# A decoder layer on one core: head factors a head ahead, a batched last norm, a separate buffer for the third group's maxima, and an expert product moved ahead of four transposes

## The reference, cut to what matters

```
u = x * (1 + sc1) + sh1                      # sc1, sh1, ... = silu(c) @ w_ada + b_ada, six rows of 1024
z = u @ w_in                                 # the columns of all branches, split below
y_gla = gla(q, k, v, r, lr @ w_gate)         # 4 heads, 8 chunks of 64 tokens: b = cumsum(log a);
    att   = (q exp(b - ref)) (k exp(ref - b))^T, masked
    state = state * exp(b_last) + (k exp(b_last - b))^T v
    o     = att v + (q exp(b)) state ; o = rms_norm(o) * norm_g * silu(r)
y_att = three groups of dilated attention (8 heads each, head size 64), softmax per group,
        groups merged by their maxima and sums
x1 = layer_norm(alpha * x + g1 * (merge(y_gla, y_att) @ w_out))
u2 = x1 * (1 + sc2) + sh2
y  = top-1 group, top-2 of 32 SwiGLU experts on u2
out = layer_norm(alpha * x1 + g2 * y)
```

## Time and profile before

| what | value |
| --- | --- |
| median of three runs | 1498.01 us |
| the profiled execution: its time, its span | 1499.82 us, 1497.5 us |
| mean granted TensorE clock | 0.932 |
| busy PE, DVE, ACT, POOL | 88%, 69%, 46%, 23% |
| chain that ended last, by engine | PE 79%, DVE 11%, ACT 3%, DMA 2%, SPq 2%, issue 2% |
| linear attention heads, from the first `gp` to the first `yT` transpose | 189.7 to 383.0 us |
| first expert product to the last | 871.1 to 1452.0 us |
| after the last product | 1452.0 to 1497.5 us |

### The profile page before, as it was taken

How to read it: one execution, slowest core, us unless ns; L and a number is a source line. 1 busy time by engine, 2 the same in 40 slices (tenths; PEclk the granted TensorE clock), 3 DMA queues, 4 the chain that set the end, 5 groups by cost and what they waited for, 6 DMA issues and landing times.

```text
span 1497.5 us, 18092 instructions
## 1 busy us (share of the span) xinstructions
PE 1318.7 (88%) x6280; PEld 1069.7 (71%) x6280; DVE 1032.6 (69%) x1144; ACT 690.0 (46%) x844; POOL 351.0 (23%) x212
## 2 busy tenths in 40 slices
PE   3899976886899997999989469999999999999970
PEld 2678764554689887888768458888888888888850
DVE  6755855445344332343779768999999999999957
ACT  2322233123333332445230337777767777777721
POOL 0000000000000000000000133655556555655430
PEclk8899988977999998999999579999999999999985
DMA  9965321101220313225341949999999999999922
GB/s 351 334 238 218 120 85 42 43 1 41 72 70 27 115 57 114 70 71 183 124 163 74 405 162 353 372 373 363 366 378 352 372 379 370 375 372 358 355 80 112
DMA packets 73970, 318.63 MB, mean 213 GB/s; under 512 B 14978, under 2 KB 15138, under 8 KB 49088
## 3 DMA queue, kind: packets, MB, share of 16 engines
q1 hardware_dynamic: 57728, 284.41, 51.2%
q0 software_dynamic: 15328, 30.39, 6.5%
q10 hardware_dynamic: 864, 3.15, 0.5%
HBM read 315.67 MB, written 31.04 MB: 232 GB/s over the span
## 4 chain that ended last, share of the span: by engine, by line
PE 79%; DVE 11%; ACT 3%; DMA 2%; SPq 2%; issue 2%; DVEq 0%; POOLq 0%; ACTq 0%
PE ps L931 12%; PE ps L933 12%; PE ps L932 12%; PE ps L725 10%; PE ps L726 10%; PE ps L727 10%; PE ps L852 2%; PE ps L921 2%; PE ps L894 1%; PE ps L810 1%; PE ps L830 1%; PE ps L827 1%; PE ps L818 1%; PE ps L948 1%; PE ps L864 1%
## 5 line engine op out<-in xcount | busy, mean ns | idle before, releaser
L1607 DVE TENSOR_TENSOR w_lo<-w_raw,w_hi 128x2048 fp32r<-128x2048 f32 x192 | 433.2, 2285 | 41.0 <-ACT w_hi L1134 41.0
L1134 ACT CAST w_hi<-w_raw 128x2048 fp32r<-128x2048 f32 x192 | 357.6, 1919 | 0.0
L931 PE MATMUL ps<-w_hi,xT_hi 128*128 128x512 f32 x512 | 207.5, 405 | 2.4 <-DVE xT_lo L1620 2.4
L664 POOL DMA_INDIRECT y_d<-yb,ui x32 | 162.7, 5084 | 171.9 <-DVE yb L1615 147.5
L933 PE MATMUL ps<-w_hi,xT_lo 128*128 128x512 f32 x512 | 201.7, 394 | 0.0
L932 PE MATMUL ps<-w_lo,xT_hi 128*128 128x512 f32 x512 | 200.7, 392 | 0.0
L1222 DVE TENSOR_TENSOR d_lo<-d_raw,d_hi 128x1024 fp32r<-128x1024 f32 x96 | 115.1, 1222 | 82.4 <-ACT d_hi L1002 81.8
L725 PE MATMUL ps<-uT_hi,d_hi 128*128 128x512 f32 x384 | 156.0, 406 | 1.3 <-DVEq L1272 1.2
L727 PE MATMUL ps<-uT_hi,d_lo 128*128 128x512 f32 x384 | 151.4, 394 | 0.0
L726 PE MATMUL ps<-uT_lo,d_hi 128*128 128x512 f32 x384 | 151.2, 394 | 0.0
L933 PEld LDWEIGHTS ps<-w_hi,xT_lo 128*128 128x128 f32 x512 | 96.9, 189 | 21.7
(11 more groups left out here) (304 smaller groups left out, 2201.4 us busy)
## 6 DMA issues: line engine op xcount, KB each, us to landing
w_raw<-in SPq DMA_DIRECT2D x192, 1024.0 KB, 7.4
d_raw<-in SPq DMA_DIRECT2D x96, 512.0 KB, 3.3
ada_buf<-in SPq DMA_DIRECT2D x8, 2048.0 KB, 10.4
ada_w<-in SPq DMA_DIRECT2D x8, 1024.0 KB, 14.0
att_d<-Og POOLq DMA_DIRECT2D x2, 1056.0 KB, 7.4
O<-att_d POOLq DMA_DIRECT2D x2, 1056.0 KB, 8.0
x_in<-in SPq DMA_DIRECT2D x1, 2048.0 KB, 13.8
brep_d<-bvec_d POOLq DMA_DIRECT2D x2, 1024.0 KB, 18.6
```

What stands on the lines that cost most here:

```text
L664: pool.indirect_dma_start(y_d, bass.IndirectOffsetOnAxis(ap=idxs[s], axis=0), yb[s][:, :], None, bounds_check=S - 1, oob_is_err=False, com ...
L931: pe.matmul(dst, a_hi[:, k, :], hi[:, w], start=(k == 0), stop=False)
L1134: act.copy(w_hi[n % NHI][:, :], w_raw[j][:, :]).then_inc(w_hi_rdy, 1)
L1607: dve.tensor_tensor(w_lo[j][:, :], w_raw[j][:, :], w_hi[n % NHI][:, :].bitcast(f32), ALU.subtract).then_inc(w_lo_rdy, 1)
```

## The change

Five things are done.

1. **Head factors.** `gla_args` is cut in two: the arguments (`gla_args`) and the exponentials with their four products (`gla_fac`). Head 0's stand among the `ra` blocks (after blocks 17 and 20 of 24); those of head h+1 stand in head h, the arguments between `gla_kv` and `gla_o`, the factors behind `gla_o`. One block lies between `gla_kv` and `gla_o`, two behind. To clear the memory that the arguments use, the modulation sums take blocks 1 to 16 and their loads come earlier.
2. **Third group.** Its maxima and sums go to a buffer `stat2`; only ACT's first `PV` of the group waits for the store of the second, and DVE copies `stat2` into `Og[1]` at the end.
3. **Experts.** In the first stage the gate product of chunk 1 stands ahead of the transposes of h of chunk 0, with the splits that it needs ahead too.
4. **y_d.** `y_d` starts as alpha times x1 (ACT scales the first norm's gain and bias), so the zero stores, the separate x1 store and its load at the end are gone.
5. **Tail.** No addition; statistics of all four tiles first, one rsqrt for the four; DVE finishes three tiles with two operations each; ACT and POOL (two products, L700 and L701 of the changed kernel) finish the fourth.

```diff
     for n, o in enumerate(sum(gla_q, [])):
-        if n and n % 4 != 2 and halves:
+        if n and halves:
...
+        if n == 17:
+            z(("gp", 0, None))
+            steps.append(("gla_args", 0))
+        if n == 20:
+            steps.append(("gla_fac", 0))
     for h in range(GH):
-        z(("gp", h, None))
-        steps.append(("gla_args", h))
-        zs_next(g0[3 * h]), zs_next(g0[3 * h + 1])
         steps.append(("gla_kt", h))
         steps.append(("gla_kv", h))
-        zs_next(g0[3 * h + 2])
+        if h + 1 < GH:
+            z(("gp", h + 1, None))
+            steps.append(("gla_args", h + 1))
+        zs_next(g0[3 * h])
         steps.append(("gla_o", h))
+        if h + 1 < GH:
+            steps.append(("gla_fac", h + 1))
+        zs_next(g0[3 * h + 1]), zs_next(g0[3 * h + 2])
...
-        ada_after = {11: (2,), 13: (3,), 15: (4,), 19: (5, 6), 23: (7,)}
+        ada_after = {10: (2,), 12: (3,), 14: (4,), 15: (5, 6), 19: (7,)}
...
-            pool.dma_start(x1_d[P * t:P * t + P, :], x1[:, t, :]).then_inc(x1_st, 16)
+            pool.dma_start(y_d[P * t:P * t + P, :], x1[:, t, :]).then_inc(x1_st, 16)
...
-        for t in range(NT):
-            pool.dma_start(y_d[P * t:P * t + P, :], xg[1][:, :]).then_inc(y_zero, 16)
...
+        pool.wait_ge(xn_rdy, 1)
+        r = ya[:, NT - 1, :]
+        link(pool.tensor_tensor(r, r, ln2gb[:, 0, :], ALU.mult))
+        pool.tensor_tensor(r, r, ln2gb[:, 1, :], ALU.add).then_inc(last_rdy, 1)
...
                 down(n + 2, i)
-            h_transposes(c)
+                h_transposes(c)
             if not final:
...
                 product(bank(0), xT_hi[1 - s], xT_lo[1 - s], n + 4, i)
+                if first:
+                    h_transposes(c)
...
+            if kind == "wo" and q == 0:
+                act.wait_ge(ln_used, 1)
+                act.mul(ln_g[:, :], ln_g[:, :], ALPHA).then_inc(ln_alpha, 1)
+                act.mul(ln_b[:, :], ln_b[:, :], ALPHA).then_inc(ln_alpha, 1)
...
-                if j == 0 and g == 2:
-                    act.wait_ge(att_st[0], 16)
...
-                                          bias=nmx[a % 2][:, t:t + 1], accum_out=og[:, t, j, DH + 1:DH + 2])
+                                          bias=nmx[a % 2][:, t:t + 1],
+                                          accum_out=stat2[:, 1, t, j:j + 1] if g == 2 else og[:, t, j, DH + 1:DH + 2])
...
                 act.wait_ge(pv_ps, a + 1)
+                if a == 2 * HPG:
+                    act.wait_ge(att_st[0], 16)
...
             if first:
-                todo = [5, 6, 7, 8]
+                todo = [6, 7, 8]
             sigmoid(c)
+            if first:
+                x_split(c + 1, 1 - s)
...
-                if j == 0 and g == 2:
-                    dve.wait_ge(att_st[0], 16)
...
+            elif kind == "PV" and a == 3 * HPG - 1:
+                dve.wait_ge(p_sb, 3 * HPG)
+                dve.wait_ge(att_st[0], 16)
+                dve.tensor_copy(Og[1][:, :, :, DH:DH + 2].rearrange("p t h c -> p c t h"), stat2[:, :, :, :]).then_inc(stat_rdy, 1)
...
-            link(dve.scalar_tensor_tensor(out=r, in0=x1b[:, t, :], scalar=ALPHA, in1=ya[:, t, :], op0=ALU.mult, op1=ALU.add))
-            row_stats(r, rs4[:, t:t + 1])
...
+            dve.bn_stats(bn4[:, 12 * t:12 * t + 6], ya[:, t, 0:512])
+            link(dve.bn_stats(bn4[:, 12 * t + 6:12 * t + 12], ya[:, t, 512:1024]))
+            link(dve.bn_aggr(mv4[:, 2 * t:2 * t + 2], bn4[:, 12 * t:12 * t + 12]))
...
+        rsqrt(rs4, ssq, rs_t)
...
+        for t in range(NT - 1):
+            r = ya[:, t, :]
+            link(dve.scalar_tensor_tensor(out=r, in0=r, scalar=mv4[:, 2 * t:2 * t + 1], in1=ln2gb[:, 0, :],
+                                          op0=ALU.subtract, op1=ALU.mult))
+            dve.scalar_tensor_tensor(out=r, in0=r, scalar=rs4[:, t:t + 1], in1=ln2gb[:, 1, :],
+                                     op0=ALU.mult, op1=ALU.add).then_inc(fin_rdy, 1)
```

More of the change, by code:

```diff
@@ L539, in _ @@
         sp.dma_start(ln2gb[:, 1, :], ln2_b.broadcast_to([P, D])).then_inc(ln2_in, 16)
-        sp.wait_ge(w_used, NRAW * last + (NRAW + 4))
-        sp.dma_start(x1b[:, :, :], x1_d.rearrange("(t p) d -> p t d", p=P)).then_inc(x1_back, 16)
         sp.wait_ge(w_used, NRAW * last + (NRAW + 6))
@@ L546, in _ @@
             sp.dma_start(ya[:, t, :], y_d[P * t:P * t + P, :]).then_inc(fin_in[t], 16)
+        sp.wait_ge(fin_rdy, 2)
+        sp.dma_start(out[P:2 * P, :], ya[:, 1, :]).then_inc(out_st, 16)
+        sp.wait_ge(last_rdy, 1)
+        sp.dma_start(out[P * NT - P:P * NT, :], ya[:, NT - 1, :]).then_inc(out_st, 16)
     @block.gpsimd
@@ L667, in _ @@
         gather(0, 0)
-        pool.wait_ge(y_zero, 16 * NT)
+        pool.wait_ge(x1_st, 16 * NT)
         gather(1, 1)
@@ L1151, in stage @@
             if first:
-                todo = [5, 6, 7, 8]
+                todo = [6, 7, 8]
             sigmoid(c)
+            if first:
+                x_split(c + 1, 1 - s)
             for m in todo[:2]:
                 w_split(m, i)
-            if not final:
+            if not first and not final:
                 x_split(c + 1, 1 - s)
@@ L1175, in _ @@
         w_split(4, 0)
+        w_split(5, 0)
         x_split(0, 0)
@@ L1192, in _ @@
             act.dma_start(ya[:, t, :], y_d[P * t:P * t + P, :]).then_inc(fin_in[t], 16)
-        for t in range(NT):
-            act.wait_ge(nmr_rdy, t + 1)
-            act.activation(r2[:, t, :], r2[:, t, :], ACT.Identity, bias=nmr[:, t:t + 1], scale=rs4[:, t:t + 1]).then_inc(xn_rdy, 1)
-            if t:
-                act.wait_ge(fin_rdy, t)
-                act.dma_start(out[P * t - P:P * t, :], r2[:, t - 1, :]).then_inc(out_st, 16)
-        act.wait_ge(fin_rdy, NT)
-        act.dma_start(out[P * NT - P:P * NT, :], r2[:, NT - 1, :]).then_inc(out_st, 16)
+        act.wait_ge(nmr_rdy, 1)
+        t = NT - 1
+        act.activation(ya[:, t, :], ya[:, t, :], ACT.Identity, bias=nmr[:, t:t + 1], scale=rs4[:, t:t + 1]).then_inc(xn_rdy, 1)
+        for t in (0, 2):
+            act.wait_ge(fin_rdy, t + 1)
+            act.dma_start(out[P * t:P * t + P, :], ya[:, t, :]).then_inc(out_st, 16)
         act.wait_ge(out_st, 16 * NT)
@@ L1296, in evac @@
                     dve.tensor_tensor(mods[:, 1, :], lnt[0][:, :], mods[:, 1, :], ALU.add)
-                    link(dve.tensor_tensor(mods[:, 2, :], ln_g[:, :], mods[:, 2, :], ALU.mult))
+                    dve.tensor_tensor(mods[:, 2, :], ln_g[:, :], mods[:, 2, :], ALU.mult).then_inc(ln_used, 1)
+                    dve.wait_ge(ln_used, 1)
                     dve.wait_ge(out_rdy, i + 1)
@@ L1628, in stage @@
             if first:
-                todo = [5, 6, 7, 8]
-            for m in todo[:2]:
+                todo = [None, None, None, 6, 7, 8]
+            for m in todo[:2] if not first else []:
                 w_rest(m, i)
@@ L1633, in stage @@
                 x_rest(c + 1, 1 - s)
-            for m in todo[2:3]:
+            for m in todo[2:3] if not first else []:
                 w_rest(m, i)
@@ L1655, in _ @@
         w_rest(4, 0)
+        w_rest(5, 0)
         stage(0, 0, first=True)
```

43 lines of the change are left out of this document (21 added, 22 removed).

## The result

The changed kernel takes 1420.45 us (median of 4 runs, 1416.15 to 1420.77), the kernel before 1498.32 beside it: a ratio of 0.9473, with a 95% interval of 0.9456 to 0.949. Forecast were 1419.6 us. The profiled execution has a span of 1418.7 us (1497.5 before).

What follows compares the result with a forecast made beforehand. PE was taken to bound nearly all of the span, through its waits, its lower clock and the tail. Gains of 50.3 + 9.1 + 5.3 + 13.7 = 78.4 us from 1498.0 gave 1419.6 us, range 1405 to 1438.

Steps and rivals of the forecast that it cites:

- the 5 us added for the clock: Heads: 5 us added to the section's time in case light small products alone make PE's clock fall.
- the middle of 2.1 and 4.2 us: Heads, small products L810: time taken midway, as nothing showed whether clock or issue limits them.
- the bounds of 38 and 58: Heads: gain at least 38 us with slow L810 and a fall in each, at most 58 with fast L810, none.
- the clock term: Third attention group: one fall of PE's clock, 1.6 us, gained besides the wait of 7.5 us.
- DVE's three tiles, two operations of 1.25 each, 7.5: Tail: DVE finishes three tiles with two operations of 1.25 us each, 7.5 us in all.
- the third rival: Tail: POOL and DVE take turns, POOL's time coming on top of DVE's; 1424 to 1425 us, chance 0.15.
- POOL's guessed 5.8 us: Tail: time of POOL's two products, 2.9 us each, taken as three fills.
- The 0.3 us guessed for scalars read from memory: Tail: 0.3 us more for DVE's operations on its three tiles, whose scalars are read from memory.
- The likeliest case: Whole kernel: the summed gains hold, 1412 to 1428 us around the forecast, chance 0.45.
- Modulation loads late: Rival, `ra` section: waits move there through a late load or DVE behind at every block; 1436 us, chance 0.08.
- A steady loop with a new wait: Rival, experts: a wait for DVE in every chunk; at 3 us a chunk 1513 us, slower, chance 0.02.
- The clock falling in every head: Rival, heads: the clock falls in each and L810 stays at 4.2 us; gain 38, time 1432 us, chance 0.15.

## Why the prediction was right, point by point

- **Part 1, 50.3 forecast, 55.6 measured.** Its steps held nearly to the microsecond: the last `ra` block ends at 199.6 (199.8), head 0's state products at 204.8 (205.5), the three heads take 98.1 (97.7), the rest to `yT` 24.65 (24.5). The mis-sized term is the 5 us added for the clock. I feared that light products alone make it fall; in the heads it fell only behind the waits of 4.68 and 2.58 us. The first had its own 1.6 in the `ra` section; the second cost 1.7 that the heads' sum had not counted, and got back from L810, taken as the middle of 2.1 and 4.2 us and measured at 2.46, 0.7 less in each head. So L810 hung mostly on the clock. Between the bounds of 38 and 58 this part came out near the upper one. Outside the heads, something like the fear did happen: in the second attention group the clock fell behind small products with a wait of only 0.60 us, at 3.2 us in this execution and 1.6 in the second one. That the small products are the cause is not shown, since the same ones left the clock at 1.00 before.
- **Part 2, 9.1 forecast.** The 8.3 between the marks of the table hold the fall just named. From marks around the place it gained 10.4, and 9.1 by undoing it. The wait is as forecast (7.5, 7.3); the clock term, forecast at 1.6, was 2.9 and 1.8.
- **Part 3, 5.3 forecast.** 4.9 between marks, 4.4 to 5.2 by undoing it. The new wait for `hb` is 2.1, not 3. The gain lasted to the tail, as the earlier trace rows had let expect.
- **Part 4, 0 forecast.** No difference.
- **Part 5, 13.7 forecast, 10.1 measured.** The step that failed is "DVE's three tiles, two operations of 1.25 each, 7.5": DVE's six take 11.7 us (1403.69 to 1415.35), because POOL's products take turns with it. This is the mechanism of the third rival. Its price was too high: it put POOL's guessed 5.8 us on top of DVE's, but the products alone are 2.33 each and 4.0 us came on top. The 0.3 us guessed for scalars read from memory came out as 0.2 in the sum (1.28 an operation against 1.25). The likeliest case held in heads, group and experts and this rival in the tail; the chance of 0.15 for it was too low, since both sides were known to read two tensors in SBUF at once. The page "GPSIMD Engine Reference" of the Trainium skill had the better answer twice. Its section 3.1 puts a `tensor_tensor` add on GpSimd at 1.96 times VectorE's time; the trace agrees, since 2.33 against 1.22 is 1.9. Its section 8 names contention with VectorE instructions that have two SBUF inputs; the trace agrees, with 2.0 us more for each of the two that met POOL's, and with one input in PSUM it is gone.
- **The other rivals.** Modulation loads late: neither PE nor DVE waits for such a load among the `ra` blocks. A steady loop with a new wait: none; from 905 to 1375 us the clock is 1.00 and PE is busy 469 of 470 us. The clock falling in every head: no, though with the remainders moved it fell in one more.
- **The whole.** The account of the waits held in parts 1 to 4, but that the total came out at 78.8 against 78.4 is luck: +5.3 and +1.3 at two waits and their clock, +1.2 at `yT`'s transposes, -3.2 for an unforeseen fall, -0.4 in the experts and -3.6 in the tail.

## What to carry to other kernels

Work that one engine needs late but whose inputs are ready early belongs in front of it by a full stage; what it then costs is not zero but the length of the queue that it delays, and that can be added up row by row beforehand. Before giving GpSimd a share of VectorE's last work, count the inputs that both read in SBUF: here a quarter of the tiles handed over made the tail 1.9 us longer than leaving all to VectorE. One operand in PSUM removed the conflict, and the tail was then as long as with all on VectorE. Judge a term of a few microseconds from marks close to it, since two executions of the same kernel reached the tail 3.2 us apart, and look at the clock between the marks as well as at the waits.
